# Two encoder layers on one core: the even mixer's input projections as three-term split products

## The reference, cut to what matters

```python
def mixer_even(h, conf_state, ssd_conv_state, ssd_state, w_in, conf_w, conf_b, ...):
    proj = h @ w_in                       # h: rmsnorm(x) * gain, 640 x 1024
    a_val, a_gate, z, xbc, dt_raw = jnp.split(proj, ...)   # 512, 512, 512, 1024, 8 columns
    a_glu = a_val * jax.nn.sigmoid(a_gate)
    a_conv, new_conf_state = causal_dwconv(a_glu, conf_state, conf_w, conf_b)    # 31 taps
    a_out = jax.nn.silu(layernorm(a_conv, ln_g, ln_b))
    xbc_c, new_xbc_state = causal_dwconv(xbc, ssd_conv_state, xbc_w, xbc_b)      # 4 taps
    xbc_c = jax.nn.silu(xbc_c)
    # then dt = softplus(dt_raw + bias), the SSD scan in chunks, gate with silu(z), norm, @ w_out
```

## Time and profile before

| what | value |
| --- | --- |
| median of 3 runs | 1749.54 us (1748.26 to 1749.71) |
| profiled execution, its own time | 1749.37 us |
| profiled execution, span of the trace | 1747.5 us |
| PE busy | 1707.0 us, 98% |
| DVE busy | 1059.2 us, 61% |
| ACT busy | 683.6 us, 39% |
| POOL busy | 370.2 us, 21% |

### The profile page before, as it was taken

One profiled execution on the slowest core, in us unless ns is written; L12 is line 12 of the kernel. 1 busy time (PEld: TensorE's weight loads), 2 busy tenths in 40 slices (PEclk: granted clock), 3 DMA queues, 4 the chain that ended last, 5 costly groups with the idle time before them and its releaser, 6 DMA issues.

```text
span 1747.5 us, 27689 instructions
## 1 busy us (share of the span) xinstructions
PE 1707.0 (98%) x11360; PEld 1546.2 (88%) x11360; DVE 1059.2 (61%) x1717; ACT 683.6 (39%) x1219; POOL 370.2 (21%) x289
## 2 busy tenths in 40 slices
PE   7999998999999999999999999999999999999999
PEld 6566556897999999999989898679889999999999
DVE  3699867647677647465654325645566774655564
ACT  4111243334534525253542134533543453444352
POOL 3012100211104223132213133100110241414240
PEclk9999999999999999999999999999999999999999
DMA  8222330142304140403133123402421313212212
GB/s 261 103 79 97 98 118 11 49 193 97 109 25 140 39 136 23 134 26 127 36 129 73 74 73 138 170 27 76 191 73 43 127 40 112 70 61 94 86 67 91
DMA packets 39674, 162.30 MB, mean 93 GB/s; under 512 B 9384, under 2 KB 10280, under 8 KB 25600
## 3 DMA queue, kind: packets, MB, share of 16 engines
q1 hardware_dynamic: 32240, 124.59, 21.0%
q0 software_dynamic: 7312, 35.98, 5.7%
HBM read 149.87 MB, written 10.42 MB: 92 GB/s over the span
## 4 chain that ended last, share of the span: by engine, by line
PE 92%; DVE 4%; ACT 2%; issue 1%; DMA 0%; POOL 0%; SPq 0%; DVEq 0%; ACTq 0%
PE G L940 68%; PE S L940 12%; PE Q L940 11%; ACT work L1726 1%; PE Q L1640 1%; DVE rstd L2337 0%; ACT rstd L1726 0%; DVE ev_low L2586 0%; DMA ring<-in_w_mk 0%; DVE stats L2616 0%; DVE resid L2868 0%; ACT h_split L1726 0%; DVE stats L2985 0%; PE Q L1347 0%; DVE work L2629 0%
## 5 line engine op out<-in xcount | busy, mean ns | idle before, releaser
L940 PE MATMUL G<-ffn_rows,w_split 128*128 128x320 f32 x2160 | 329.8, 309 | 0.0
L940 PEld LDWEIGHTS G<-ffn_rows,w_split 128*128 128x128 f32 x2160 | 320.1, 188 | 0.0
L1726 ACT ACTIVATE w_split<-ring 128x512 fp32r<-128x512 f32 (+2 forms) x224 | 159.1, 711 | 316.7 <-PE G L940 208.3
L940 PE MATMUL G<-front,ring 128*128 128x128 f32 (+2 forms) x832 | 222.7, 429 | 10.9 <-DMA ring<-in_w_mk 9.1
L940 PEld LDWEIGHTS G<-front,ring 128*128 128x128 f32 x832 | 132.6, 193 | 99.7 <-issue 95.7
L856 POOL TENSOR_TENSOR mkT<-ring 128x512 f32<-128x512 f32 x72 | 97.7, 1362 | 564.5 <-DMA ring<-in_w_up 381.5
L940 PE MATMUL G<-h_split,w_split 128*128 128x320 f32 x1344 | 200.9, 310 | 1.2 <-DVE w_split L2352 0.9
L940 PEld LDWEIGHTS G<-h_split,w_split 128*128 128x128 f32 x1344 | 197.5, 188 | 1.9 <-issue 1.3
L940 PE MATMUL G<-g_split,w_split 128*128 128x320 f32 x1056 | 163.7, 310 | 0.1
L940 PEld LDWEIGHTS G<-g_split,w_split 128*128 128x128 f32 x1056 | 156.6, 188 | 1.6 <-DVE w_split L2841 1.3
L2708 DVE TENSOR_TENSOR w_split<-ring,w_split 128x512 fp32r<-128x512 f32 (+1 forms) x124 | 105.9, 856 | 60.3 <-ACT w_split L1726 59.1
(11 more groups left out here) (351 smaller groups left out, 2801.1 us busy)
## 6 DMA issues: line engine op xcount, KB each, us to landing
ring<-in_w_up SPq DMA_DIRECT2D x44, 1024.0 KB, 4.7
ring<-in_w_down SPq DMA_DIRECT2D x48, 256.0 KB, 2.6
ring<-in_w_down SPq DMA_DIRECT2D x32, 320.0 KB, 2.9
front<-in_mem_k POOLq DMA_DIRECT2D x8, 1024.0 KB, 6.8
front<-in_mem_v POOLq DMA_DIRECT2D x8, 1024.0 KB, 11.1
ring<-in_w_mk SPq DMA_DIRECT2D x4, 1024.0 KB, 6.2
ring<-in_w_mv SPq DMA_DIRECT2D x4, 1024.0 KB, 11.0
ring<-in_w_glu SPq DMA_DIRECT2D x4, 1024.0 KB, 8.9
```

What stands on the lines that cost most here:

```text
L940: return nc.tensor.matmul(out, lhsT, rhs, start=start, stop=stop, **kw)
L1726: return nc.scalar.activation(*a, **k)
```

## The change

All 20 tiles of `glu`, `xbc` and `z` become split products. ACT writes the high part of each weight tile (`mix_weights(q)`, q = 0 to 19, 128x1024) into a buffer of two tiles, POOL writes the low part over the ring slot (`mix_low(q)`), ACT writes a high part of each row block of `h` (`mix_high_row`) into `mix_hi`, and DVE the low part into `ev_lo` (eight instructions ahead of the glu loop). `mix_hi` lies where the residual `x` lies, so `x` is fetched again from DRAM, by POOL's queue after the last z tile, and the first residual add waits for it. The dt columns use high and low rows one after the other (32 matmuls for 16). Tiles 0 and 1 first take the two terms with high rows, then the third. The load of the SSD state moves behind the last `mix_low`. DVE runs 24 instead of 32 tap instructions after each of the first three glu pairs. The first of the four xbc taps goes from DVE to ACT (`xbc_first_tap`).

```diff
+            def mix_low(q):
+                pool.wait_ge(mix_high, q + 1)
+                src, hi, lo = mix_piece(q)
+                nc.gpsimd.tensor_tensor(lo, src, hi.bitcast(F32), ALU.subtract).then_inc(mix_split, 1)
             memory_keys(0)
+            mix_low(0)
+            mix_low(1)
             for j in range(4):
+                if j < 3:
+                    mix_low(2 * j + 2)
+                    mix_low(2 * j + 3)
                 read_wait(pool, TILE0["glu"] + 2 * j + 1)
...
             memory_keys(1)
+            mix_low(8)
+            mix_low(9)
             for j in range(KD):
+                mix_low(10 + j)
                 read_wait(pool, xbc_tile(j))
...
+            for q in range(18, 20):
+                mix_low(q)
+            pool.dma_start(h0T, dram["ssd_state"]).then_inc(state_in, 16)
+            tile_wait(pool, z_tile(3))
+            pool.dma_start(x[:, :, :], dram["x"][:, :, :]).then_inc(x_again, 16)
...
+            def mix_terms(q, terms, ends, halfway=None):
+                out = GF[mix_tile(q) % 2]
+                _, w_hi, w_lo = mix_piece(q)
+                for k in range(KD):
+                    for t in terms:
+                        if q == 0 and t < 2:
+                            pe.wait_ge(mix_rows_hi, k + 1)
+                        elif q == 0:
+                            pe.wait_ge(mix_rows, k + 1)
+                        w, rhs = ((w_hi, mix_hi[:, k, :]), (w_lo, mix_hi[:, k, :]), (w_hi, mix_low_row(k)))[t]
+                        for e in range(2):
+                            fr = slice(e * HT, (e + 1) * HT)
+                            m = mm(out[:, fr], w[:, k, :], rhs[:, fr], ...)
+            def mix_product(q, halfway=None):
+                begin(mix_tile(q))
+                pe.wait_ge(mix_split, q + 1)
+                mix_terms(q, (0, 1, 2), True, halfway)
-            projections("glu", 8, KD, rows(h), norm="mix0")
-            narrow(TILE0["dtp"], "wdt", h)
+            for q in range(2):
+                begin(mix_tile(q))
+                pe.wait_ge(mix_split, q + 1)
+                mix_terms(q, (0, 1), False)
+            for q in range(2):
+                mix_terms(q, (2,), True)
+            for q in range(2, 8):
+                mix_product(q)
+            narrow(TILE0["dtp"], "wdt", (mix_hi.bitcast(F32), ev_lo.bitcast(F32)))
...
+            def mix_weights(q):                       # ACT
+                act.wait_ge(chunk_in[c % RING], 16 * (c // RING + 1))
+                if q >= 2:
+                    tile_wait(act, mix_tile(q - 2))
+                A(hi, src, ACT.Copy).then_inc(mix_high, 1)
             memory_values(0, 0)
+            mix_weights(0)
+            mix_weights(1)
             residual_inv_std(2)
+            mix_high_row(0)
             memory_values(0, 1)
+            for k in range(1, KD):
+                mix_high_row(k)
             for j in range(4):
                 evacuate(tmp[:, j % 2, :], t0 + 2 * j, ACT.Sigmoid, out=GF)
+                if j < 3:
+                    mix_weights(2 * j + 2)
+                    mix_weights(2 * j + 3)
...
                 A(b, runs(GF[n % 2][:, SEQ:T]), ACT.Copy).then_inc(read[n % 2], 1)   # xbc_rows(j)
+                mix_weights(10 + j)
...
-                conv_taps(32 if j < 3 else 44)
+                conv_taps(24 if j < 3 else 44)
...
             for j in range(2):
                 xbc_silu(j)
+                xbc_first_tap(j + 2)
...
-                for w in range(XW):
+                for w in range(1, XW):
...
+            dve.wait_ge(x_again, 16)
             add_residual("evout", evout_rows, tmp[:, 0, :], GF, ...)
```

More of the change, by code:

```diff
@@ L265, in pr @@
             return par[0:rows, o:o + 1]
+        with nc.sbuf_tensor("mix_high", [P, KD, T], F32R) as mix_hi:
+            pass
         x = sb("resid", [P, KD, T])
@@ L474, in evout_piece, with mix_tile, mix_chunk, mix_piece @@
             return src, ev_w[:, i % 2], lo
+        MIX = [("glu", i) for i in range(8)] + [("xbc", i) for i in range(8)] + [("z", i) for i in range(4)]
+        def mix_tile(q):
+            name, i = MIX[q]
+            return z_tile(i) if name == "z" else TILE0[name] + i
+        def mix_chunk(q):
+            name, i = MIX[q]
+            return CHUNK[name] + i // 2
+        def mix_piece(q):
+            at = mix_chunk(q) % RING
+            src, lo = (w[:, at, :].rearrange("p (k n) -> p k n", k=KD)[:, :, q % 2 * P:(q % 2 + 1) * P]
+                       for w in (ring, ring_r))
+            return src, mix_w[:, q % 2], lo
+        def mix_low_row(k):
+            return ev_lo[:, k, :]
         def odout_piece(i):
@@ L1041, in narrow @@
                 pe.wait_ge(par_in if wname == "wdt" else wf_ready, 16 if wname == "wdt" else 1)
[L1042 to L1046, removed]
+                for part, rows_part in enumerate(rows_of):
+                    for k in range(KD):
+                        q, o = k % 4, PAR[wname][0] + k * NH
+                        rows, w = slice(32 * q, 32 * q + 32), par[:, o:o + 32]
+                        first, last = part == 0 and k < 4, part == len(rows_of) - 1 and k >= 4
+                        mm(out[rows, 0:512], w, rows_part[:, k, 0:512], first, last, tile_position=(0, 32 * q))
+                        m = mm(out[rows, 512:T], w, rows_part[:, k, 512:T], first, last, tile_position=(0, 32 * q))
                 m.then_inc(tile_done, 1)
@@ L1120, in _ @@
             memory_values(1)
[L1121 to L1125, removed]
+            for j in range(KD):
+                mix_product(8 + j)
+                if j == 5:
+                    conv_stat(3)
+            for j in range(2):
+                mix_product(16 + j)
             nready[0] += 4
@@ L1138, in _ @@
                 .then_inc(tile_done, 1)
-            s = chunk(CHUNK["z"] + 1)
-            for n in range(2, 4):
-                project(z_tile(n), s, n % 2 * P, KD, rows(h), halfway=h_free if n == 3 else None)
+            for j in range(2, 4):
+                mix_product(16 + j, h_free if j == 3 else None)
             RUN, CSK = NCH - 1, 64 + NH
@@ L1877, in _ @@
                     read_wait(act, t0 + 2 * (j - 2) + 1)
-                evacuate(tmp[:, j % 2, :], t0 + 2 * j, ACT.Sigmoid)
+                evacuate(tmp[:, j % 2, :], t0 + 2 * j, ACT.Sigmoid, out=GF)
+                if j < 3:
+                    mix_weights(2 * j + 2)
+                    mix_weights(2 * j + 3)
             act.wait_ge(par_in, 16)
@@ L1888, in xbc_rows, with xbc_first_tap @@
                 a, b = padded(xbcp, j, XW - 1, XPROMPT, XREQ, XW - 1)
-                A(a, G[n % 2][:, 0:SEQ], ACT.Copy)
-                A(b, runs(G[n % 2][:, SEQ:T]), ACT.Copy).then_inc(read[n % 2], 1)
+                A(a, GF[n % 2][:, 0:SEQ], ACT.Copy)
+                A(b, runs(GF[n % 2][:, SEQ:T]), ACT.Copy).then_inc(read[n % 2], 1)
+                mix_weights(10 + j)
+            def xbc_first_tap(j):
+                if j >= 2:
+                    act.wait_ge(xbc_done, j - 1)
+                else:
+                    read_wait(act, TILE0["glu"] + 5 + 2 * j)
+                read_wait(act, xbc_tile(j))
+                act.wait_ge(pads_in, 16 * 12)
+                out = (tmp[:, j % 2, 0:SEQ], runs(tmp[:, j % 2, SEQ:T]))
+                for i in range(2):
+                    A(out[i], padded(xbcp, j, 0, XPROMPT, XREQ, 0)[i], ACT.Identity, scale=pr("xw", j * XW),
+                      bias=pr("xb", j)).then_inc(first_tap, 1)
             def xbc_silu(j):
-                act.wait_ge(xconv, 2 * XW * (j + 1))
+                act.wait_ge(xconv, 2 * (XW - 1) * (j + 1))
                 A(xbcc[:, j, :], tmp[:, j % 2, :], ACT.Silu).then_inc(xbc_done, 1)
             def z_gate(j):
-                evacuate(zs[:, j, :], z_tile(j), ACT.Silu)
+                evacuate(zs[:, j, :], z_tile(j), ACT.Silu, out=GF)
+                if j < 2:
+                    mix_weights(18 + j)
             act.wait_ge(dt_abs, 1)
@@ L2393, in _ @@
             nnorm[0] += 4
+            for k in range(KD):
+                dve.wait_ge(mix_rows_hi, k + 1)
+                v.tensor_tensor(mix_low_row(k), h[:, k, :], mix_hi[:, k, :].bitcast(F32), ALU.subtract)\
+                    .then_inc(mix_rows, 1)
             def step_sizes():
```

54 lines of the change are left out of this document (38 added, 16 removed).

## The result

The changed kernel takes 1786.93 us (median of 4 runs, 1785.96 to 1788.28), the kernel before 1748.90 beside it: a ratio of 1.0217, 95% interval 1.0201 to 1.0234. It is slower by 38 us. The forecast had the direction (slower) and not the size: +17.6 forecast, and 1786.9 lies above the range's 1774. What set the time is rival 2, POOL starves, which I had given a chance of 0.10, and it cost more than I had worked out for it.

The account below looks back on a forecast made before the run. PE and DVE were both taken as full in the xbc stage, with DVE only 8.2 us ahead. Scan at 221.1 + 59.6 = 280.7, less 3.6: 277.1 against 259.49, +17.6 on 1749.4 gives 1767 us; range 1749 to 1774.

Parts of the forecast that it names:

- rival 2: POOL's subtractions get through only at gaps in DVE's taps, so PE waits at xbc tile 2: +15, 1764 us, chance 0.10.
- The start: Before the glu tiles: first row waits 2.2 us, PE starts at 50.1, tile 2 at 67.6 after a 1.8 us gap.
- From there to the xbc tiles: Glu tiles end at 109.9, dt at 114.6, memory stage unchanged except 0.8 us of waiting, xbc starts at 147.3.
- PE's own arithmetic: Twenty split tiles at 7.04 instead of 8.65 us save 32.3, dt matmuls add 2.3: PE alone would gain 30.0 us.
- What a subtraction costs DVE: Each weight subtraction on POOL beside DVE's two-input instructions makes DVE lose 2.24 us, between bounds of 0 and 2.41.
- I let one in eight go that way: One POOL subtraction in eight waits through several DVE taps instead of delaying DVE, taking 3.6 us off the forecast.
- the row at 128.12: Earlier trace row where POOL's 0.72 us operation took 3.46, standing through six DVE taps; treated as an exception.
- The sum of the convolution: DVE's sum ready at 221.1: 65.9 plus 125.3 of its work plus 29.9 for subtractions; PE idles some 31 us.
- It never has a gap: DVE works without pause from first gating to convolution sum; a glu pair costs it 16.6 us, PE needs 14.1.
- The tail, T + 59.6: From the convolution's sum (T = 221.1) to the scan: 59.6 us, scan at 280.7, or 277.1 less the exceptions.
- rival 1: POOL's subtractions cost DVE almost nothing: sum ready about 197.4, scan at 252.5, 7 us won, 1742 us, chance 0.15.
- At nothing: Second fetch of `x` (up to 20 us if uncovered) and SSD state load (a few us) were counted as free.

## Why the prediction was wrong, point by point

- *The start*: right. First glu matmul at 50.11 (forecast 50.1), tile 2 at 67.93 (67.6).
- *From there to the xbc tiles*: too early by 7 us. "Later weight parts are ready one tile ahead" did not hold: subtractions 4 and 6 waited for the end of a row of taps, and tiles 4 and 6 started after waits of 0.85 and 1.68 us for them. The dt matmuls ended at 117.55 (forecast 114.6). The memory stage, "unchanged except for a wait of 0.8", took 37.2 instead of 32.0 us: the wait of 3.4 for `rstd`, and slower matmuls behind it (the last 64 took 15.30 instead of 14.08 us). The xbc tiles started at 154.7 and not at 147.3.
- *PE's own arithmetic*: right in kind. Four tiles without a wait (208.04 to 238.94) took 28.2 us in the forecast and 30.9 in the trace, since PE was at the lower of its two clock levels (1.2 and 2.4 GHz) for part of the stretch behind a wait; the mean granted clock is 0.90 there and 0.76 in the whole xbc window.
- *What a subtraction costs DVE*: 2.24 us forecast. Where POOL gets in, it is 2.1 to 2.2 in the convolution's rows (the two runs with drains) and 2.5 in xbc's (18 taps in 13.42 instead of 8.41 us, two subtractions), so the price itself was right.
- **The step that failed** is the one behind it: "I let one in eight go that way". It let a wait of POOL be rare and six taps long at most, 3.46 us, as in the row at 128.12, and put PE's wait for low parts, before the sum, at nothing beyond the start., from which I took the price, shows POOL's subtraction starting 0.6 us before DVE's instruction. It says nothing of POOL coming into a row of 60 taps. The strict reading of the Trainium skill (SBUF — State Buffer, "Who interferes with whom"), that the one issued first keeps the port for its instruction, made me take POOL's wait as one tap long. The measured waits are 28.07 - 2.4 = 25.7 and 30.0 - 2.4 = 27.6 us, some 55 and 59 taps: in these two rows the next tap went first each time. PE stood 15.97 and 20.43 us for them, and 51.1 us for low parts in all. Of the ten operations of POOL that came into taps between 70 and 300 us of the changed kernel, five waited for the end of the row (subtractions 4, 6, 9 and 10 and the memory keys) and five got in within 0.5 us (5, 7, 16, 17 and 18). So the share of the exceptions was one in two and not one in eight, and their length was that of the row.
- *The sum of the convolution*: forecast at 221.1 by DVE's loss. Measured 213.3. In the run where POOL only writes it was ready at 196.9; of the 16.4 us between the two, DVE stood 14.5 beside POOL: 7.5 in the glu stage and at the step sizes, 2.1 at the first taps at 175, 4.9 in the sum itself. The forecast had 29.9, since it let 14 subtractions meet DVE before the sum, and here subtractions 12 to 15 came only after it. "It never has a gap" failed too: from the first gating to the sum DVE waited 9.3 us for PE (4.0 for the glu tiles, 5.3 for the dt tile at 139.85), so part of the 24 taps that moved behind the glu stage would have had room there. But PE's idle time was ended by POOL and not by the sum, which was ready 25 us before PE came to it.
- *The tail, T + 59.6*: right in size, counted from PE's matmuls of the sum. From there to the scan it took 58.80 in the changed kernel, 58.67 and 59.2 in the runs with drains; for rival 1 (55.1 forecast) the run with writes has 55.55. The second gap before z tile 1, ended by POOL, was forecast at 5 to 10 us and took 10.15.
- *At nothing*: right. No wait is ended by the second fetch of the residual (14.0 us to landing) or by the SSD state.
- *Rival 2's own size*: 1764 forecast, 1787 measured. Its chain had the scan at 274.6; it came at 297.54. It took DVE as unhurt, with the taps ended at about 195; they ended at 205.7, since DVE had stood beside POOL and had waited for PE, so xbc tile 2 started at 208.04 and not at 199.8 (8.2). Tiles 2 to 5 took 30.9 instead of 28.2 (2.7). And the chain let PE run on through six tiles and the z tiles without the mean, squares and taps of DVE and ACT, most of which this kernel's order puts behind xbc tile 5: 58.6 from there instead of 46.6 (12.0). Together 22.9 us. Had I used my own tail for it, rival 2 would have stood at 1776.5 (274.6 + 12.0 - 259.49 on top of 1749.4), outside my range. The range ended at 1774 since I took the forecast's own mechanism as the worst case.

With drains every sixteenth tap, where the forecast's premise holds, the scan starts at 278.17 (forecast 277.1) and the time is 1768.2 (forecast 1767.0). So the forecast's mechanism is sized within 1.2 us of its own case, with some luck: the exceptions I took off (3.6 us) don't occur there, and the lower price (29.9 / 2.24 = 13.4 subtractions, 13.4 x 0.14 = 1.9 us) and a tail shorter by 0.9 make up for most of them. It was the wrong mechanism for this kernel.

## What to carry to other kernels

Before giving a side job to an engine whose instructions another engine's can keep waiting, look at the row of instructions it has to get into. A trace in which it was let in once doesn't price it; look for its longest wait beside the densest row, and ask what waits for it then. Where the busy engine can do the job itself, compare its own duration (1.2 us here) with how long it stands when the other does it (2.1). And put a rival's chain through the same tail as the forecast's.

## What the runs showed of the hardware

- POOL's instruction that reads SBUF waited through up to sixty DVE taps with two SBUF inputs (28.07 and 30.0 us for an operation of 2.4), with one input as with two; POOL's write of the same elements took 0.96 us beside the same taps. The Trainium skill (SBUF — State Buffer, "Who interferes with whom") says that of POOL's instructions only those that read SBUF contend with such an instruction: the runs agree.
- It did not always wait. Beside taps of the same kind and cadence POOL got in within 0.5 us at 83.38, 98.71, 250.71, 268.61 and 272.40 of the changed kernel, and each time a tap stood for it (the 128-column tap at 83.85 took 2.49 us instead of 0.34). The record's order of starts does not tell the two cases apart (177.83 against 177.87, and POOL waited 27.6 us). What does is open.
- DVE waiting for its own last instruction, 0.12 us, kept POOL's waits short: the longest subtraction took 2.9 us with a drain every fourth tap and 5.1 with one every sixteenth. A DVE write of one column, which reads nothing, did so only at part of the places (34.1 and 21.6 us at two others), with 16 us between the fastest and the slowest run.
- A DVE instruction with one SBUF input beside which POOL got in stood as well: two first taps took 2.93 us instead of 0.79. It stood beside POOL's write too, though less: 1.69 us for the two at 64.80 in the run with writes, where the write takes 0.95.
